# A mixture-of-experts stage: rows turned once into the accumulators, square sums through the router's product, the first expert's rows gathered alone

## The reference, cut to what matters

```python
h2 = rmsnorm(x, norm2_g) * (1.0 + sc2) + sh2
g_prob = softmax(h2 @ w_group + b_group)                 # 4 groups, best one
e_logits = (h2 @ w_expert + b_expert).reshape(T, 4, 8)   # in that group: best two
order = argsort(expert); xs = h2[tok]                    # 512 slots, sorted by expert
hid = silu(ragged_dot(xs, w_gate, sizes)) * ragged_dot(xs, w_up, sizes)
out = ragged_dot(hid, w_down, sizes) * weights[order][:, None]
x = x + g2 * (zeros_like(t).at[tok].add(out))
return rmsnorm(x, final_g)
```

## Time and profile before

| | us |
|---|---|
| median of 3 runs (1275.18 to 1276.27) | 1275.25 |
| span of the profiled execution, first to last instruction | 1277.6 |
| PE busy in it | 1116.7 (87%) |
| DVE busy | 685.3 (54%) |
| ACT busy | 421.0 (33%) |
| hardware queue 1, share of 16 engines | 68.0% |

### The profile page before, as it was taken

How to read it: one execution, slowest core, us unless ns; L and a number is a source line. 1 busy time by engine, 2 the same in 40 slices (tenths; PEclk the granted TensorE clock), 3 DMA queues, 4 the chain that set the end, 5 groups by cost and what they waited for, 6 DMA issues and landing times.

```text
span 1277.6 us, 23118 instructions
## 1 busy us (share of the span) xinstructions
PE 1116.7 (87%) x9331; PEld 904.2 (71%) x9333; DVE 685.3 (54%) x1069; ACT 421.0 (33%) x532; POOL 32.8 (3%) x71
## 2 busy tenths in 40 slices
PE   9999999999999999999999999678766567666676
PEld 8999999999968999999998899533322233322232
DVE  5799988887445746557866767632112112112114
ACT  3775333345384433334644673410000000000001
POOL 0000000000000000001000000000000000000000
PEclk9999999999999999999999999889888888888889
DMA  9678988874530785550463336799999999999996
GB/s 347 225 262 301 342 299 302 305 261 158 176 128 1 263 311 198 173 174 2 179 225 132 133 141 239 305 378 416 428 427 430 427 428 430 427 430 427 428 430 259
DMA packets 99401, 362.48 MB, mean 284 GB/s; under 512 B 4160, under 2 KB 51664, under 8 KB 84112
## 3 DMA queue, kind: packets, MB, share of 16 engines
q1 hardware_dynamic: 95216, 335.06, 68.0%
q0 software_dynamic: 3984, 26.50, 5.3%
q10 hardware_dynamic: 144, 0.10, 0.0%
HBM read 360.58 MB, written 1.06 MB: 283 GB/s over the span
## 4 chain that ended last, share of the span: by engine, by line
PE 60%; DMA 23%; DVE 10%; ACT 3%; issue 2%; another core or an unknown queue 1%; SPq 0%; POOLq 0%; DVEq 0%; POOL 0%; ACTq 0%
DMA wbuf<-in_w_up 22%; PE ps L1897 16%; PE ps L1820 9%; PE ps L1783 8%; PE ps L2231 6%; PE ps L2107 4%; DVE parts L1107 3%; PE ps L1804 3%; PE ps L1829 2%; PE ps L2251 1%; PE ps L2281 1%; PE ps L1773 1%; PE ps L2014 1%; PE ps L1980 1%; DMA wbuf<-in_ffn_w_in 1%
## 5 line engine op out<-in xcount | busy, mean ns | idle before, releaser
L2231 PE MATMUL ps<-wbuf,big 128*32 128x256 f32 x2176 | 166.2, 470 | 109.4 <-DMA wbuf<-in_w_up 97.8
L1897 PE MATMUL ps<-big_parts,parts 128*128 128x256 f32 x2112 | 255.0, 282 | 1.4 <-DVE parts L1107 1.4
L1107 DVE TENSOR_TENSOR parts<-wbuf,parts 128x2048 fp32r<-128x2048 f32 x92 | 208.7, 2287 | 84.8 <-ACT parts L835 43.9
L1897 PEld LDWEIGHTS ps<-big_parts,parts 128*128 128x128 f32 x2112 | 252.3, 188 | 2.2 <-DVE parts L1107 1.4
L2231 PEld LDWEIGHTS ps<-wbuf,big 128*32 128x32 f32 x2176 | 85.5, 134 | 203.8 <-issue 98.1
L1693 DVE TENSOR_TENSOR big<-big,ps 128x128 f32<-128x128 f32 x33 | 9.5, 288 | 265.2 <-ACT big L1039 265.2
L1039 ACT ACTIVATE big<-ps 128x128 f32<-128x128 f32 x33 | 9.2, 278 | 415.7 <-PE ps L2231 415.7
L1820 PE MATMUL ps<-big_parts,parts 128*128 128x256 f32 x1088 | 132.9, 282 | 0.6 <-DVE parts L1107 0.6
L1820 PEld LDWEIGHTS ps<-big_parts,parts 128*128 128x128 f32 x1088 | 130.7, 189 | 0.8 <-DVE parts L1107 0.8
L1783 PE MATMUL ps<-parts_f,parts 128*128 128x256 f32 x704 | 98.4, 284 | 0.0
L1783 PEld LDWEIGHTS ps<-parts_f,parts 128*128 128x128 f32 x704 | 90.5, 192 | 0.1
(11 more groups left out here) (353 smaller groups left out, 1409.9 us busy)
## 6 DMA issues: line engine op xcount, KB each, us to landing
wbuf<-in_w_down SPq DMA_DIRECT2D x32, 2048.0 KB, 37.9
wbuf<-in_w_gate SPq DMA_DIRECT2D x31, 2048.0 KB, 32.6
wbuf<-in_w_up SPq DMA_DIRECT2D x31, 2048.0 KB, 37.1
wbuf<-in_ffn_w_in SPq DMA_DIRECT2D x44, 1024.0 KB, 12.1
wbuf<-in_w_ada POOLq DMA_DIRECT2D x24, 1024.0 KB, 8.6
wbuf<-in_ffn_w_out SPq DMA_DIRECT2D x22, 1024.0 KB, 5.1
wbuf<-in_w_in SPq DMA_DIRECT2D x10, 2048.0 KB, 8.8
wbuf<-in_attn_w_qkv SPq DMA_DIRECT2D x6, 2048.0 KB, 8.6
```

The source lines that it names most:

```text
L1107: nc.vector.tensor_tensor(lo, whole, hi.bitcast(F32), ALU.subtract).then_inc(done, 1)
L1897: ins = mm(ps[:, b, d * 256:(d + 1) * 256], w[pw][:, k, d * P:(d + 1) * P], h_part_of[px][:, k], start=(k == 0 and d == 0 and i == 0), sto ...
L2231: ins = mm(at, rows, gu_place[s][:, :, k, r * P:(r + 1) * P], start=(k == 0), stop=(k == KC - 1))
```

## The change

- **Square sums.** ACT squares `xT` itself, block by block, into `square_rows`, and PE multiplies the squares with a matrix `square_column` (one column of ones at place 36) into the same PSUM bank as the logits. The logit rows are then 37 wide, and the last column is the sum of squares.
- **Rows turned once, into the accumulators.** The turned rows go to banks 4 to 7 and stay there. The copies to `x_tok`, the four zero products and the additions at the end go. ACT makes scaled rows `h2_rows` in f32 in SBUF; the high and low parts are later made from those.
- **First expert alone.** As soon as the places are known, DVE makes `pick_first` (32 slots of expert 0), PE gathers its rows in f32 straight from `h2_rows`, ACT scales and shifts them, and gate/up follows. The full gather of both halves comes after.
- **Warm-up.** PE runs 16 products of zeros (128x512 bf16) while DVE routes.
- **Order after it.** The first half's gather, the first expert's down product, the spread, the register load, then the second half. The windows are counted in one operation each, and SP waits for `first_gu` directly.

Cut to its core:

```diff
+GATHER_BANK = ((3, 1, 2, 3), (3, 1, 0, 3))
+WARM_ROUTE = 16
...
-            sp.wait_ge(first_gu, 1)
             sp.wait_ge(info_ready, 1)
-            with sp.Fori(0, (N_EXP - EXPERT_SLOTS) // EXPERT_SLOTS) as j:
+            n_more = sp.value_load(info[0:1, N_EXP:N_EXP + 1], min_val=0, max_val=SEQ // WIN - 1)
+            sp.wait_ge(first_gu, n_more + 1)
+            load_gate_up(sp, 0, EXPERT_SLOTS)
+            sp.wait_ge(down_done[0], 1)
+            load_down(sp, 0, EXPERT_SLOTS)
+            for e in range(1, EXPERT_SLOTS):
+                load_next(e, e)
...
ACT
-                nc.scalar.activation(h2tok[:, c, hf * 512:(hf + 1) * 512], ps[:, q, :], ACT.Square,
-                                     accum_out=small[:, 288 + q:289 + q]).then_inc(row_sq, 1)
+            for b in range(4):
+                act.wait_ge(x_ready, 4 * 5 + b + 1)
+                nc.scalar.activation(square_rows[:, 2 * b:2 * b + 2], xT[:, 2 * b:2 * b + 2], ACT.Square).then_inc(row_sq, 1)
+            act.wait_ge(logit_done, 1)
...
-                nc.scalar.activation(high_at(q), rows, ACT.Identity, scale=scale).then_inc(h2_hi, 1)
+                nc.scalar.activation(turned_at(h2_rows, q), rows, ACT.Identity, scale=scale).then_inc(rows_scaled, 1)
-            for q in range(4):
-                nc.scalar.activation(x_tok[:, q // 2, (q % 2) * 512:(q % 2 + 1) * 512], ps[:, q, :], ACT.Copy).then_inc(rows_kept, 1)
+            for k in range(KC):
+                act.wait_ge(gather_pe, k // HALF * HALF + HALF)
+                modulated(xs[:, k, 0:WIN], ps[:, (3, 1)[k // HALF], k * WIN:(k + 1) * WIN], k).then_inc(early_ev, 1)
+            for c in range(TC):
+                nc.scalar.activation(high_rows(c), rows_of(h2_rows, c), ACT.Copy).then_inc(h2_hi, 1)
...
+            gathered(0, range(KC))
+            gathered(1, range(2))
             act.wait_ge(spread_pe, 1)
...
DVE
+            for c in range(TC):
+                V.tensor_scalar(pick_first[:, c], slot_no[:, 0:WIN], sm(FIRST_AT + c), sm(FIRST_MASK + c), ALU.is_equal, ALU.mult).then_inc(early_pick, 1)
...
             pick_half(0)
-            for q in range(4):
-                V.scalar_tensor_tensor(out=turned_at(h2_low, q), in0=ps[:, q, :].rearrange("t (p k) -> t p k", k=KC), ...
+            for c in range(TC):
+                V.tensor_tensor(rows_of(h2_low, c), rows_of(h2_rows, c), high_rows(c).bitcast(F32), ALU.subtract).then_inc(h2_lo, 1)
...
-            def add_rows(c, hf):
-                at = x_tok[:, c, hf * 512:(hf + 1) * 512]
-                V.tensor_tensor(at, ps[:, 4 + 2 * c + hf, :], at, ALU.add).then_inc(fin_add, 1)
...
PE
+            for b in range(3):
+                logit_part(b)
+            for b in range(2):
+                square_part(b)
+            logit_part(3)
+            for b in range(2, 4):
+                ins = square_part(b)
+            turn_rows(0)
...
+            turn_rows(1)
+            for _ in range(WARM_ROUTE):
+                mm(ps[:, 0, :], zero_half[:, 0:P], zero_half, start=True, stop=True)
...
+            for k in range(KC):
+                gather_first(k)
+            for k in range(KC):
+                ins = first_gate_up(k)
+            ins.then_inc(first_gu, 1)
...
+            gather(0, range(3))
+            pe.wait_ge(gather_ev, 2)
+            gather(0, (3,))
...
+            pe.wait_ge(gather_ev, 6)
+            down_part(0, 0, 0, 1, first_hidE, first_pair)
+            pe.wait_ge(spread_ready, 1)
+            for q in range(2):
+                mm(ps[:, 1 - q, :], ones, spread[:, q], start=True, stop=True).then_inc(spread_pe, 1)
+            pe.wait_ge(spread_ev, 2)
             pe.wait_ge(info_ready, 1)
             n_more = pe.value_load(info[0:1, N_EXP:N_EXP + 1], min_val=0, max_val=SEQ // WIN - 1)
...
+            gather(1, range(1, 3))
+            pe.wait_ge(gather_ev, KC + 2)
+            gather(1, (3,))
```

More of the change, by code:

```diff
@@ L1045, in _ @@
                 act.wait_ge(more_done, w + 1)
-            gathered(1)
+            gathered(1, range(2, KC))
             act.wait_ge(info_ready, 2)
@@ L1657, in _ @@
             ins.then_inc(spread_ready, 1)
-            link(V.tensor_tensor(sm(32, 32), sm(32, 32), sm(START, 32), ALU.subtract))
-            link(V.tensor_scalar(sm(96, 32), sm(32, 32), float(WIN), None, ALU.is_gt))
-            for w in range(2, SEQ // WIN):
-                link(V.scalar_tensor_tensor(out=sm(96, 32), in0=sm(32, 32), scalar=float(w * WIN), in1=sm(96, 32), op0=ALU.is_gt, op1=ALU.add))
-            V.tensor_copy(info[:, 32:64], small[0:1, 96:128]).then_inc(info_ready, 1)
-            pick_half(1)
@@ L2181, in _, with part @@
             accumulate_by_bank(part_terms(unit_parts("out1"), 4, lambda px, k: merged_part[px][:, 4 + k]))
[L2184 to L2194 removed]
+            def part(w, rows, b, first, last):
+                for h in range(2):
+                    ins = mm(ps[h * HALF_ROWS:(h + 1) * HALF_ROWS, 1, 0:SEQ], w(2 * b + h), rows[:, 2 * b + h], start=first, stop=last)
+                return ins
@@ L2232, in gate_up_product, with gather_first, first_gate_up, gather @@
                 return ins
-            pe.wait_ge(rows_kept, 4)
+            def gather_first(k):
+                for c in range(TC):
+                    ins = mm(ps[:, (3, 1)[k // HALF], k * WIN:(k + 1) * WIN], h2_rows[:, c, k * P:(k + 1) * P], pick_first[:, c], start=(k % HALF == 0 and c == 0), stop=(c == TC - 1),
+                             skip_group_check=True)
+                ins.then_inc(gather_pe, 1)
+            def first_gate_up(k):
+                pe.wait_ge(early_ev, k + 1)
+                return gate_up_product(k, xs[:, k, 0:WIN], 0)
+            pe.wait_ge(rows_scaled, 4)
+            pe.wait_ge(early_pick, TC)
             pe.wait_ge(gu_loaded[0], 32)
             for k in range(KC):
-                pe.wait_ge(gather_ev, k + 1)
-                ins = gate_up_product(k, xs[:, k, 0:WIN], 0)
+                gather_first(k)
+            for k in range(KC):
+                ins = first_gate_up(k)
             ins.then_inc(first_gu, 1)
-            pe.wait_ge(spread_ready, 1)
-            for q in range(2):
-                mm(ps[:, 1 + q, :], ones, spread[:, q], start=True, stop=True).then_inc(spread_pe, 1)
-            pe.wait_ge(half_ready, 2)
-            for b in range(4, 8):
-                mm(ps[:, b, :], zero_half[:, 0:P], zero_half, start=True, stop=False, skip_group_check=True)
+            def gather(half, pairs):
+                for pair in pairs:
+                    for k in range(2 * pair, 2 * pair + 2):
+                        for i, (rows, c) in enumerate(((rows_high, 0), (rows_high, 1), (rows_low, 0), (rows_low, 1))):
+                            ins = mm(ps[:, GATHER_BANK[half][pair], k % 2 * 256:(k % 2 + 1) * 256], rows(k, c), pick[half][:, c], start=(i == 0), stop=(i == 3))
+                        ins.then_inc(gather_pe, 1)
+            pe.wait_ge(pick_ready, TC)
+            pe.wait_ge(h2_hi, TC)
+            pe.wait_ge(h2_lo, TC)
+            gather(0, range(3))
+            pe.wait_ge(gather_ev, 2)
+            gather(0, (3,))
             def combine(q, stop=False):
```

237 lines of the change are left out of this document (114 added, 123 removed).

## The result

The changed kernel took **1282.7 us** (median of 7 runs, 1280.42 to 1284.48), the kernel before in the same session 1275.89 us (7 runs, 1273.94 to 1278.44). The ratio is **1.0039, 95% interval 1.0026 to 1.0053**: slower by 5 us, where 1274.0 with a range up to 1276.8 was forecast. (The quotient of the two medians is larger, 1.0053 or 6.8 us, at the upper end of that interval.) The profiled execution of the changed kernel took 1280.43 us, with a span of 1277.9.

A forecast was written before the change was run, and what follows sets the result against it. The prediction took the end of the weight-transfer stream, opened by two gates, as the bound. Its terms, -0.5 for the stream and -0.7 at the end, took 1275.25 to 1274.05, rounded to 1274.0 us; range 1271.5 to 1276.8.

The forecast's parts named there:

- two gates in a row: First gate/up, then expert 1's gate/up release refills; freeing only the first leaves the queue empty 4.5 us behind expert 3's load.
- The routing stage: Before the first gather: DVE starts scaling 0.2 us later (bounds -0.3, +0.8), at 811.9; `gather_first` starts at 818.2.
- The end without `add_rows`: End of the kernel: squaring from PSUM one addition sooner, scalings no longer behind four additions, -0.7 us.
- the term taken at 0: End of the kernel: the scaling now reads PSUM, costing between 0 and +0.3 us, taken at 0.
- the full clock for `gather_first` and gate/up: First expert's products at 2.4 GHz: gather 3.8 us, gate/up 3.74; at 1.2 GHz the gather would take 6.7.
- the first gate: First expert's gate/up done, releasing the first refill: issue at 825.8 instead of 830.86, 5.1 us earlier.
- my first rival: The clock falls before or in `gather_first`: second gate at 850.2, time 1277.6, or 1278 with slower DVE steps; chance 0.08.
- the second gate: Expert 1's gate/up done, releasing the second refill: issue at 846.7 instead of 846.42; load 4's stream gains 0.5 us.
- gate/up of expert 1 at 3.7: Expert 1's gate/up product, ahead of the second refill: 3.7 us, from 842.9 to 846.6.
- The term at zero: pauses of PE's queue: Inside expert 1's gate/up: the 0.93 us of issue pauses taken as gone.
- The third gate: Third refill: stays in place relative to the second if the 4.9 us branch pause stays; no term.
- rival 2: PE's queue pauses go, including the long branch: saves 1.1 us, 1272.9, or 1271.9 with a shorter chain; chance 0.22.

The follow-up runs named there:

- e8: The changed kernel with the start's 20 products written as 10 of twice the columns, equal work; 1281.85 us, ratio 1.0020 to the kernel before.
- e9: e4 with the start's 20 products written as 5 of 512 columns; 1273.57 us, ratio 0.9971 to the kernel before.
- e10: The changed kernel, order kept, with e1's zero products and the start's products as 5 of 512 columns; 1277.23 us, ratio 1.0000 to the kernel before.
- e1: The changed kernel with 22 zero products instead of 16 before the mask and 4 more behind the place counts; 1281.03 us, ratio 1.0026.
- e2: The changed kernel with two f32 products of 512 columns between the second half's gather and expert 1; 1280.6 us, ratio 1.0029.
- e3: The changed kernel reordered: spread, second half's gather, first down product, register load last; 1279.26 us, ratio 1.0012 to the kernel before.
- e5: The changed kernel without its 16 zero products in the routing stage; 1283.31 us, ratio 1.0048 to the kernel before.
- e4: The changed kernel with the order of e3 and the zero products of e1; 1275.98 us, ratio 0.9994 to the kernel before.
- e7: e4 with one zero product after each product pair of the first gather; 1278.99 us, ratio 1.0004 to the kernel before.
- e6: The kernel before with 22 zero products in the routing stage and 8 behind the position products; 1279.34 us, ratio 1.0003.

## Why the prediction was wrong

**What held.** The mechanism of two gates in a row: freeing the first alone only opens a hole behind load 3. In the trace of after the queue falls under 100 GB/s at 840.2 and the refill is issued at 847.18; from the first logit pass that is +38.9 to +45.9, where +37.3 to +41.8 was forecast (842.2 to 846.7 in the clock of before). The hole is 7.0 us long instead of 4.5, because both of its gates came late. The routing stage was even better than its term (DVE starts at +5.70 where +6.98 was forecast, `gather_first` at +12.06 where +13.28 was). The end without `add_rows` gives 18.9 - 18.1 = 0.8 us, forecast 0.7, as e8, e9 and e10 show it; the four scalings take 2.73 us from PSUM after and took 2.74 before, so the term taken at 0 is right. The pieces between the gates are right to 0.2 us: from the start of the first half's gather to the down product 6.35 us (forecast 6.2), from there to the second half 5.78 (5.8).

**The step that failed: the full clock for `gather_first` and gate/up.** The two took 3.73 and 3.66 in e10 and 5.11 and 5.55 after: 3.3 us at the first gate. The early start gave 1.4 of it back, so the first refill missed its forecast by 1.8 (+22.72 for +20.88). I had argued from the length of PE's gaps, 2.0 us at most against the 2.8 after which the clock had been seen low. After has gaps of 1.48 and 0.91 us there, shorter than those, and the clock fell 2.3 us into the gather. e1 shows that the length of the gaps is no safe ground at all: PE busy without such a gap, and the clock fell during the gather itself. Over the runs, in the one profiled execution of each, the five kernels with 16 or no zero products in the routing stage all had it fall before the first gather had ended (after, e2, e3, e5, e8); of the five with 22 and 4, one did (e1). The same gather passes take 7.00 us without the 16 zero products (e5) and 5.11 with them (after), while e1 and e4 have the same instructions up to there with either outcome (4.26 and 3.73 us). This was my first rival, with a chance of 0.08; it was the likely case. It put the second gate at 850.2, that is +45.3, close to the measured +45.88, though by other terms; its price of 1277.6 was still too low, since it too had nothing for the pause in the last expert. What lets the clock fall in one execution and not in another stays open.

**The same step a second time: gate/up of expert 1 at 3.7.** It took 5.35, the clock being 0.50 for 3.4 us of it: 1.65. The row that should have warned stands in the forecast's own sum: ahead of that product PE now waits for ACT and POOL. e10 has its half clock a little earlier, in the second half's gather (4.38 for 24 passes instead of 3.08). Its gate/up takes 4.37, but at the full clock. Busy time by stretch of e10_warm_layout:
```profile
837.80:841.10 3.30, 2.93 (x15) 2.63 (x13) 0.00 (x0) 2.18 (x5) 0.00 (x0) 0.50 0.83 353
841.50:847.00 5.50, 4.31 (x66) 2.47 (x66) 0.00 (x0) 0.29 (x1) 1.08 (x3) 1.00 0.02 6
```
The 0.7 us above 3.66 are thus not the clock's; the passes thin out from 843.25 to 844.0, where the granted clock is 1.00. Its second gate is only 2.7 us sooner than after's, although its first is 3.3 sooner.

**The term at zero: pauses of PE's queue.** I took the pause inside expert 1's gate/up as gone and gave nothing in its place. The branch of 2.97 us put 0.8 back (2.68 us ahead of gate/up against 1.86 in e10, which has no branch over 0.36). Together: 1.8 + 1.65 + 0.8 is the 4.1 us by which the second refill missed its forecast (+45.88 for +41.78), to 0.2.

**The third gate: the gain of rival 2, without its condition.** The long branch didn't go. It took 5.24 us after, for 4.89 before, but it stands at 862.8, one expert later, behind the third refill (858.40, 11.2 us behind the second instead of 15.6). So the loss of 1.1 us went, at the price that rival 2 had for it, for a reason that it didn't name. Of 4.4 us at the gate 3.3 should then be left at the last gate/up product; 2.8 are, the rest being within the spread named under the table.

**A term that was not in the sum.** The pause in the last expert, 2.0 us. Its place follows the number of passes issued ahead of it. Counted in passes from the start of the last gate/up product it is 66 after (64 and two of `combine`), 56 in e1 (10 passes more in the code), 62 in e2 (4 more), 65 in e3, 56 in e4 (10 more than e3, so 55 by the count) and 48 in e7 (8 more than e4). By that count e8, e9 and e10 should have it at 86, among the passes of the down product, and e5 (16 fewer) at 82; it isn't seen there. Expert 2's gate/up product has a pause that follows the same count. PE after, expert 2's gate/up:
```profile
851.85 3.65 PE L2266 MATMUL ps<-wbuf,big 128*32 128x256 f32 x60 [0.16 <-issue]
857.74 0.62 PE L2266 MATMUL ps<-wbuf,big 128*32 128x256 f32 x4 [2.24 <-issue]
```
PE of e7_down_last_pad, the same product:
```profile
849.62 2.75 PE L2267 MATMUL ps<-wbuf,big 128*32 128x256 f32 x42 [0.25 <-issue]
855.40 1.50 PE L2267 MATMUL ps<-wbuf,big 128*32 128x256 f32 x22 [3.03 <-issue]
```
It stands at 60 after and in e3, 50 in e1 and e4, 56 in e2 and 42 in e7; and in the kernel before with e6's 30 products, the pause in expert 1's gate/up moved from 54 to 24 and that in expert 3's from 60 to 30. The pause thus belongs to a place in the stream of instructions and not to an operation: these positions show that, and the ratio of e8 leans the same way. What makes PE stop at that place no run shows: the fetch of code that the expectations of e8 and e9 name was a guess of mine. Nor does a run show why no pause is seen at 82 and 86; ahead of the down product PE waits 0.47 us for DVE (in e5 1.11 for the weights).

**The sum in ratios.** After is at 1.0039. Moving the pause is worth 0.0019 (after to e8) to 0.0023 (e4 to e9); the order 0.0027 (after to e3) and 0.0029 (e10 to e9); the zero products 0.0018 where the clock held (e3 to e4). These add up to 0.0064 to 0.0070, for the 0.0068 from 1.0039 to e9's 0.9971. The step from e4 to e9 isn't the last expert's pause alone: the gap ahead of expert 1's gate/up also went from 2.88 to 1.76 us, of which 0.5 came back in the product (4.20 at a clock of 1.00). Each ratio is uncertain by 0.0013, so a difference of two by some 0.0018: the order's is clear of that, in both pairs, the other two lean on the traces as well. After and e3 were not timed in one session, nor were e4 and e9; e9 and e10 were, and they share everything but the order, so that pair is the firm one. With the first gather's clock and the pause mended and the order kept (e10) the change brings nothing that can be measured (1.0000): the second gate is at +43.2 against +41.5, and the shorter end and the full queue behind it make up for that.

## What to carry to other kernels

A low clock cost nothing here where another engine covered the products (first refill at +25.94 with it, +25.87 in e6 without), and 3.3 us once the change had taken that cover away (5.11 and 5.55 us after, 3.73 and 3.66 in e10): cost the products on a shortened path at the clock that the rows of that stretch show, not at the clock that is hoped for. Where two gates stand in a row, move what isn't needed behind the second one before freeing the first; here the order alone decided between no gain (e10) and one of 0.29% (e9). And when a kernel's last stage shows a pause without a releaser, change the number of instructions ahead of it, at equal work, as e8 did (18.1 us to the end instead of 20.0), before believing any comparison within 2 us.

## What the chip did that I had not expected

- The clock fell at 818.7 in e1 with PE busy at 3.66 of the 3.70 us before, and stayed at 1.00 through the same gather in e4, e9 and e10.
- A pause in straight code, which lengthens the last expert's products by 2.0 to 2.8 us and moves pass for pass with the code's length.
- The long branches go with the code's length too: one of 4.0 to 5.2 us on this line in before, after, e1 to e4 and e7, none over 0.36 in e5, e6, e8, e9 and e10. Where the branch is short, PE pauses inside expert 3's gate/up product instead, 5.09 us in e5 after 15 passes, 4.15 and 4.70 us in e8 and e10 after 19, with four passes fewer in the code ahead of these two than in e5. What sets the length of a pause (0.93 us before and 3.31 in e6, in the same product) no run here separates.
